# Another order of the weight loads in a two-layer diffusion block with 32 experts a layer

## The chip, the core and the metric

The kernel runs on one core of a Trainium2 chip. Its engines are TensorE (PE, matrix products), VectorE (DVE), ScalarE (ACT), GpSimd (POOL) and SyncE (SP), which issues most of the transfers. The metric is the device time of one execution in microseconds, lower is better. All data is float32, all products are full float32 products.

## What is computed

Two layers over 256 latent tokens and 256 context tokens of width 1024. Each layer: a modulation vector from the conditioning (`silu(c) @ w_mod + b_mod`), a modulated RMS norm, one input projection split among four mixers (A a bidirectional mLSTM, B global attention, C windowed attention, D neighbourhood attention), a gated sum of the branches and an output projection; then a second norm and a mixture of 32 experts:

```python
def layer(x, l):
    h = rms_norm(x, norm1_g[l]) * (1 + sc1) + sh1
    y = sum(sigmoid(gate[i]) * (branch[i](h @ w_in[l]) @ w_branch[l, i]) for i in range(4)) @ w_out[l]
    x = x + ga1 * y
    t = rms_norm(x, norm2_g[l]) * (1 + sc2) + sh2
    expert, w = top2_in_best_group(sigmoid(t @ w_router))          # 2 of 32 for each token
    for e in range(32):                                            # tokens gathered by expert
        ys = (silu(xs @ e_gate[l, e]) * (xs @ e_up[l, e])) @ e_down[l, e]
    return x + ga2 * scatter_add(w * ys)
```

In layer 1 only the latent tokens go on after the mixers. The result is a final RMS norm.

## The kernel before

Each layer runs through the same stages, with one set of buffers. SBUF holds a ring of six slots of 2 MB (`ring`); slots 0 to 2 take the weights of the dense part in turn, slots 3 to 5 (`ext`) hold operands and results of the dense part and become slots for experts later. A plan written out ahead (`plan_dense`) numbers every dense product group; `dense_full` counts them, and a transfer into a slot waits for the number of the group that used the slot last. `blocks[l]` is the list of a layer's dense weight transfers, sorted by when their slot comes free; SP issues them in that order from one queue, each behind its wait.

**Start of a layer.** Four row blocks of `w_mod` (2 MB each, order `MOD_ORDER`) give shift and scale of the first norm: `modulation_parts(n)`, then `modulation_row(n)` on TensorE, evacuated by ScalarE (`part_evac`, `mod_evac`). Before, the blocks go to slots 0, 1, 2 and again 0, so that the fourth waits for the first product. The tokens (`X`, two transfers of 1 MB) stand in SP's queue behind the third block. In layer 0 ScalarE's order is part 0, part 1, row 0, part 2, row 1, four squares of the tokens, root, part 3, rows 2 and 3. In layer 1 it is all parts and rows, then the scaling of the fetched expert outputs (`scale_first`) and the squares; DVE adds the outputs (`add_output`) behind that. The fetched outputs come by eight gathers on POOL's queue (`fetch_outputs`), after the last scatter of the experts has landed; two of the four token tiles go to the tensor HT.

**Mixers.** Stages A, D, B, C in this order. A stage has items (a pair of heads and a token tile); layer 1 has eight items a stage, so nine steps in D, B and C. Between the parts of an item TensorE does filling work, dealt to steps by `due(l, b, i)`: in D queries and keys for B, the output products of A (`value`) and the gates of D; in B the same for C. Before, `due` deals D, B and C by length (in layer 1 a query group counts 4, a key group 2, a value group 1, a gate group 2). The neighbourhood bias comes in two halves through one buffer: the second half is loaded by POOL after item 3 has used the first (`bias_used`), and item 4 needs it. DVE norms and turns B's queries and keys in `prepare_normed`, whose steps follow from the step of the last key group.

**Experts.** Expert e uses gate, up and down weights of 2 MB each. The ring holds two experts (slot 3 x parity + 0, 1, 2). Two more matrices are loaded ahead into memory that is free during the choice: the gate weights to HT after the last router product, the up weights to the first 4096 columns of `scr` after the last rank product. Before, these are those of the last expert, 31. SP issues in order: up and down of 1, gate, up and down of 0, gate of 1 (after the normed tokens are stored in DRAM), the two overlay loads, constants for the next layer (PICK, MODA, G1), and then in a loop gate, up and down of e + 2 as soon as expert e's product with the same slot is done (`g_full`, `u_full`, `y_full`). In layer 1 (`TILED`) an expert's down product runs after the next expert's gate and up products, and the queue's order is shifted to match. POOL gathers an expert's rows (`xe_full`) and scatters its results.

## Time and profile before

| | us |
|---|---|
| median of 3 runs | 2692.15 (2687.77 to 2692.79) |
| profiled execution | 2690.23 |
| its span | 2688.6 |
| TensorE busy | 2408.3 (90%) |
| DVE busy | 1025.4 (38%) |
| ScalarE busy | 501.5 (19%) |
| GpSimd busy | 230.8 (9%) |
| bytes moved | 614.75 MB, 229 GB/s over the span |
| chain of waits | TensorE 66%, DMA 23%, DVE 7% |

The chain of waits is followed back from the last instruction to whatever released each step; its shares say which engine or transfer held the end at each time. A group in the timeline carries in brackets the idle time ahead of it and what ended it. "Landing" is the time from the issue of a transfer to its semaphore. TensorE runs at one of two granted clocks, 1.2 or 2.4 GHz, shown as 0.5 or 1.0 (PEclk).

### The profile page before, as it was taken

Reading aid. Unit: us, or ns where it says so; the run is one execution under the profiler, and the core shown is the slowest. Engines: PE = TensorE matmul, PEld = TensorE weight load, DVE = VectorE, ACT = ScalarE, POOL = GpSimd, SP = SyncE. Lnnn points to the kernel's source line nnn. Section 1 sums busy time; section 2 is a strip of 40 time slices with the busy share of each in tenths; the row PEclk is TensorE's granted clock in tenths of the full one; section 3 lists DMA queues with packets and bytes.
Section 4 is the critical chain, followed back from the end, with each engine's and each line's share of the span. In section 5 each row is a group of like instructions: output and inputs, shape, how many; then the busy total and the mean of one; then the engine's idle time right before and its main releaser. Section 6 shows DMA issues by size and latency. Waiting matters only on the chain.

```text
span 2688.6 us, 45465 instructions
## 1 busy us (share of the span) xinstructions
PE 2408.3 (90%) x19016; PEld 1450.8 (54%) x19017; DVE 1025.4 (38%) x2392; ACT 501.5 (19%) x992; POOL 230.8 (9%) x392
## 2 busy tenths in 40 slices
PE   5999999999998979999999489999999788887884
PEld 2455545454444467777667156567676444444442
DVE  2226545365674332322222232435557521111112
ACT  2023222222231101111001112222223111101011
POOL 3000001000000011111110100000000011111111
PEclk8989999999999879999999798999999889999997
DMA  9111118234344479999999521133456779999993
GB/s 300 63 63 63 48 63 315 92 114 115 101 133 138 172 279 413 409 404 391 386 390 351 219 75 63 63 110 91 155 179 192 288 308 414 410 416 413 413 397 137
DMA packets 151925, 614.75 MB, mean 229 GB/s; under 512 B 16145, under 2 KB 20785, under 8 KB 135249
## 3 DMA queue, kind: packets, MB, share of 16 engines
q1 hardware_dynamic: 127138, 558.01, 54.5%
q0 software_dynamic: 24688, 55.39, 6.7%
q8 instruction: 66, 1.08, 0.2%
q14 instruction: 33, 0.27, 0.0%
HBM read 596.39 MB, written 42.11 MB: 237 GB/s over the span
## 4 chain that ended last, share of the span: by engine, by line
PE 66%; DMA 23%; DVE 7%; issue 2%; ACT 1%; POOL 0%; SPq 0%; DVEq 0%; POOLq 0%; ACTq 0%
DMA ring<-in_e_down_dram 21%; PE bank L1469 12%; PE bank L1349 11%; PE bank L1339 7%; PE bank L1733 5%; PE bank L1482 5%; PE score_banks L1750 4%; PE score_banks L1770 3%; PE bank L1640 2%; PE score_banks L1518 2%; PE bank L1542 2%; PE turned_banks L1528 2%; PE score_banks L1755 2%; PE bank L1726 2%; PE bank L1647 1%
## 5 line engine op out<-in xcount | busy, mean ns | idle before, releaser
L1469 PE MATMUL bank<-HT,ring 128*128 128x512 f32 (+1 forms) x1024 | 343.3, 490 | 0.4 <-ACT ring L1041 0.4
L1349 PE MATMUL bank<-ring,HT 128*128 128x512 f32 (+1 forms) x800 | 299.1, 530 | 0.0
L1733 PEld LDWEIGHTS bank<-scr,ring 128*64 128x64 f32 x7936 | 279.2, 138 | 15.5 <-issue 14.7
L1733 PE MATMUL bank<-scr,ring 128*64 128x80 f32 x7936 | 284.6, 234 | 2.1 <-DVE scr L2477 1.1
L1726 PE MATMUL bank<-ring,scr 128*64 128x256 f32 x1984 | 229.1, 384 | 40.7 <-DMA ring<-in_e_up_dram 20.1
L1469 PEld LDWEIGHTS bank<-HT,ring 128*128 128x128 f32 x1024 | 192.0, 192 | 124.0 <-issue 111.3
L1349 PEld LDWEIGHTS bank<-ring,HT 128*128 128x128 f32 x800 | 150.9, 192 | 133.8 <-issue 127.8
L1726 PEld LDWEIGHTS bank<-ring,scr 128*64 128x64 f32 x1984 | 140.2, 138 | 132.5 <-DMA ring<-in_e_gate_dram 37.2
L1339 PE MATMUL bank<-HT,ring 128*128 128x512 f32 (+1 forms) x512 | 196.2, 542 | 1.9 <-ACT HT L1041 1.9
L1770 PE MATMUL score_banks<-ring,scr 128*64 128x512 f32 x512 | 135.3, 676 | 37.7 <-DMA ring<-in_e_down_dram 36.0
L1339 PEld LDWEIGHTS bank<-HT,ring 128*128 128x128 f32 x512 | 97.1, 192 | 92.0 <-issue 88.4
L1296 ACT ACT_TABLE_LOAD x64 | 82.1, 1283 | 327.7 <-DVE scr L2518 152.1
L1041 ACT ACTIVATE ring<-bank 128x512 f32<-128x512 f32 (+1 forms) x122 | 62.4, 522 | 418.1 <-PE bank L1469 218.2
L1296 ACT ACTIVATE scr<-bank 128x320 f32<-128x320 f32 (+1 forms) x64 | 26.3, 411 | 604.9 <-PE bank L1733 321.8
L1750 PE MATMUL score_banks<-ring,scr 128*64 128x512 f32 x512 | 125.4, 635 | 14.4 <-DMA ring<-in_e_down_dram 13.6
L2129 DVE SCALAR_TENSOR_TENSOR scr<-ring,csil,scr 128x512 f32<-128x512 f32 x160 | 112.8, 747 | 0.6 <-DMA ring<-in_w_mod_dram 0.3
L2495 DVE TENSOR_TENSOR scr<-scr,bank 128x320 f32<-128x320 f32 x32 | 15.6, 488 | 242.2 <-PE bank L1733 242.2
L1213 ACT ACTIVATE scr<-turned_banks 128x1024 f32<-128x1024 f32 (+1 forms) x72 | 63.5, 882 | 208.8 <-PE turned_banks L1528 208.8
L2483 DVE COPY scr<-score_banks 64x512 f32<-64x512 f32 x64 | 44.0, 687 | 149.9 <-PE score_banks L1770 149.4
L1224 ACT ACTIVATE scr<-score_banks,nms 128x512 f32<-128x512 f32 (+1 forms) x144 | 87.0, 609 | 72.6 <-DVE nms L2270 72.6
L1770 PEld LDWEIGHTS score_banks<-ring,scr 128*64 128x64 f32 x512 | 41.6, 153 | 107.2 <-issue 88.7
L1482 PE MATMUL bank<-ring 128*128 128x512 f32 (+1 forms) x256 | 89.2, 497 | 5.6 <-DVE ring L2101 5.6
(277 smaller groups left out, 2678.7 us busy)
## 6 DMA issues: line engine op xcount, KB each, us to landing
ring<-in_e_down_dram SPq DMA_DIRECT2D x64, 2048.0 KB, 26.5
ring<-in_e_up_dram SPq DMA_DIRECT2D x62, 2048.0 KB, 27.8
ring<-in_e_gate_dram SPq DMA_DIRECT2D x62, 2048.0 KB, 27.5
ring<-in_w_in_dram SPq DMA_DIRECT2D x34, 2048.0 KB, 8.6
ring<-in_w_mod_dram SPq DMA_DIRECT2D x32, 1024.0 KB, 5.1
ring<-in_w_mod_dram SPq DMA_DIRECT2D x8, 2048.0 KB, 17.0
ys<-consts POOLq DMA_DIRECT2D x1, 10240.0 KB, 35.8
ring<-in_w_branch_dram SPq DMA_DIRECT2D x4, 2048.0 KB, 7.8
```

The lines of the kernel that those rows point to most:

```text
L1213: act.activation(PTP[:, :, 0:w], PT_[:, :, 0:w], ACT.Copy).then_inc(pair_pt, 1)
L1224: last = act.activation(PB[:, hf, 0:512 - lo], SP_[:, hf, lo:512], ACT.Exp, bias=nms[:, at + hf:at + hf + 1], scale=0.125, accum_out=rsum[ ...
L1296: act.activation(SE[:, 0:hw], ps[2][:, 0:hw], ACT.Silu).then_inc(sg_ready, 1)
L1339: m = pe.matmul(bank[:, 0:cols], w[:, k, j * P:j * P + P], HT[:, k, 0:cols], start=k == 0, stop=k == KT_D - 1)
L1349: m = pe.matmul(bank[:, 0:width], HT[:, k, t * P:t * P + P], w[:, k, 0:width], start=k == 0, stop=k == KT_D - 1)
L1469: m = pe.matmul(bank[:, 0:NQ], w[:, k, (ft % 4) * P:(ft % 4) * P + P], HT[:, k, 0:NQ], start=k == 0, stop=k == KT_D - 1)
L1482: m = pe.matmul(bank[:, 0:NQ], wb[:, k, ft * P:ft * P + P], OT[b][:, k, 0:NQ], start=k == 0, stop=k == 3)
L1726: m = pe.matmul(ps[bank][hf * HALF:hf * HALF + cap, 0:256], XTv[:, k, :], w[:, k, hf * 256:hf * 256 + 256], start=k == 0, stop=k == KT_D - 1)
L1733: m = pe.matmul(ps[bank][rows_, f * cap:f * cap + cap], w[:, k, f * P + hf * HALF:f * P + hf * HALF + HALF], XTv[:, k, :], start=k == 0, s ...
L1750: m = pe.matmul(ps[4][hf * HALF:hf * HALF + HALF, :], hv[:, f, 0:HALF], w[:, f, hf * 512:hf * 512 + 512], start=f == 0, stop=f == 3)
L1770: m = pe.matmul(ps[4][hf * HALF:hf * HALF + HALF, :], lhs, w[:, f, hf * 512:hf * 512 + 512], start=f == 0, stop=f == 3)
L2129: m = dve.scalar_tensor_tensor(out=acc, in0=x, scalar=c, in1=acc, op0=ALU.mult, op1=ALU.add)
```

## The change

- The two overlay buffers take gate and up of expert 1 instead of 31. SP's order becomes: up of 2, down of 1, expert 0's three, gate of 1 (overlay), gate of 2, the constants, up of 1 (overlay, after the first gather has landed), then gate and up of 3 and down of 2 behind expert 0, down of 3, and a loop from 4 on. Ring slots of gate and up are thereby shifted by one expert: the last even expert ends in slots 3 and 4, the last odd one in 0 and 1.
- The four row blocks of a layer's start go to slots 3, 4, 2, 0, the first projection block (mq) to slot 1, all free without a product of the same layer. In layer 1, SP waits for all gathers of the outputs ahead of the fifth block.
- The tokens are loaded by ScalarE's queue, after its first activation.
- `due` deals the groups of layer 1's stages D and B by number instead of by length.

```diff
@@ -216,10 +216,9 @@
 def due(l, b, i):
 
     steps, n = stage_steps(l, b), len(fill_groups(l, b))
-    if b == "A":
+    if b == "A" or (l == L - 1 and b != "C"):
         return range(n * i // steps, n * (i + 1) // steps)
-    last = l == L - 1
-    length = {"val": 1, "gat": 2, "gq": 4 if last else 2, "wq": 4 if last else 2, "gkv": 2 if last else 1, "wkv": 2 if last else 1}
+    length = {"val": 1, "gat": 2, "gq": 2, "wq": 2, "gkv": 1, "wkv": 1}
     size = [length[name[:3]] for name, _ in fill_groups(l, b)]
     at = [sum(size[:k]) * steps // sum(size) for k in range(n)]
     return range(sum(1 for a in at if a < i), sum(1 for a in at if a <= i))
...
@@ -579,8 +578,9 @@
 
         for l in range(L):
             qt = q_tiles(l)
-            expert = EXPERTS * l - 1
-            user = [(-2, (s, v) if l else None) for s, v in ((g_full, expert), (u_full, expert), (y_full, 2 * expert))]
+            done = EXPERTS * l
+            user = [(-2, (s, v) if l else None) for s, v in ((g_full, done), (u_full, done), (y_full, 2 * done - 2),
+                                                         (g_full, done - 1), (u_full, done - 1))]
             todo = []
 
...
@@ -623,7 +623,7 @@
 
             for n in range(4):
                 at = 512 * MOD_ORDER[n]
-                add_block((l, "mod", n), kview(w_mod, at, at + 512), 512, "mod_p", n + 1)
+                add_block((l, "mod", n), kview(w_mod, at, at + 512), 512, "mod_p", n + 1, (3, 4, 2, 0)[n])
             for name, n in (("mq", 4), ("mk", 4), ("mv", 4), ("mo", qt), ("nq", 4), ("nk", 4), ("nv", 4)):
                 add_in(name, n)
             add_gates("A")
@@ -719,12 +719,12 @@
                 for at, (dst, src, wait, arrived) in enumerate(blocks[l]):
                     if wait:
                         sp.wait_ge(*wait)
+                    if l and at == 4:
+                        for t in range(4):
+                            sp.wait_ge(yg_full[t], 32 * l)
                     sp.dma_start(dst, src).then_inc(arrived, 16)
                     if (l, at) == (0, 0):
                         sp.dma_start(PICK, ins["consts"][:, N_CONST + N_LATE:]).then_inc(pick_loaded, 16)
-                    if (l, at) == (0, 2):
-                        sp.dma_start(X[0:HALF, :, :], ins["x"][0].rearrange("(t p) d -> p t d", p=HALF)).then_inc(x_loaded, 16)
-                        sp.dma_start(X[HALF:P, :, :], ins["ctx"][0].rearrange("(t p) d -> p t d", p=HALF)).then_inc(x_loaded, 16)
 
                 def load_expert(c, e, par):
 
@@ -736,23 +736,17 @@
                     sp.dma_start(slot_view(3 * par + c, 512 if c < 2 else D), src).then_inc(w_full[3 * par + c], 16)
 
                 sp.wait_ge(mg_done, 32 * (l + 1))
-                for c in (1, 2):
-                    load_expert(c, 1, 1)
+                load_expert(1, 2, 1)
+                load_expert(2, 1, 1)
                 for (s, v), slot in last_users[l]:
                     sp.wait_ge(s, v)
                     load_expert(slot, 0, 0)
                 sp.wait_ge(dense_full, G[l, "h2t", 7] + 1)
+                sp.wait_ge(dense_full, G[l, "router", 3] + 1)
+                sp.dma_start(SECOND_GATE, ins["e_gate"][l, 1].rearrange("(p k) n -> p k n", p=P)).then_inc(second_gate_loaded, 16)
                 sp.wait_ge(h2_stored, 64 * (l + 1))
-                load_expert(0, 1, 1)
-
-                def whole(name):
-
-                    return ins[name][l, EXPERTS - 1].rearrange("(p k) n -> p k n", p=P)
-
-                sp.wait_ge(dense_full, G[l, "router", 3] + 1)
-                sp.dma_start(LAST_GATE, whole("e_gate")).then_inc(last_gate_loaded, 16)
-                sp.wait_ge(dense_full, G[l, "rank", 2] + 1)
-                sp.dma_start(LAST_UP, whole("e_up")).then_inc(last_up_loaded, 16)
+                load_expert(0, 2, 1)
+
                 sp.wait_ge(dest_ready, l + 1)
                 if l + 1 < L:
                     sp.dma_start(PICK, ins["consts"][:, N_CONST + N_LATE:]).then_inc(pick_loaded, 16)
@@ -762,42 +756,36 @@
                     sp.dma_start(G1, ins["final_g"].partition_broadcast(P)).then_inc(next_loaded, 16)
 
                 eb = l * EXPERTS
+                sp.wait_ge(dense_full, G[l, "rank", 2] + 1)
+                sp.wait_ge(xe_full[0], 8 * eb + 16)
+                sp.dma_start(SECOND_UP, ins["e_up"][l, 1].rearrange("(p k) n -> p k n", p=P)).then_inc(second_up_loaded, 16)
+
+                def load_hidden(after, e, par):
+
+                    sp.wait_ge(g_full, eb + after + 1)
+                    load_expert(0, e, par)
+                    sp.wait_ge(u_full, eb + after + 1)
+                    load_expert(1, e, par)
+
+                def load_down(after, e, par):
+
+                    sp.wait_ge(y_full, 2 * (eb + after + 1))
+                    load_expert(2, e, par)
+
+                load_hidden(0, 3, 0)
+                load_down(0, 2, 0)
                 if not TILED[l]:
-                    def reload(i, j, hidden_too):
-
-                        if hidden_too:
-                            sp.wait_ge(g_full, eb + 2 * i - 1 + j)
-                            load_expert(0, 2 * i + j, j)
-                            sp.wait_ge(u_full, eb + 2 * i - 1 + j)
-                            load_expert(1, 2 * i + j, j)
-                        sp.wait_ge(y_full, 2 * (eb + 2 * i - 1 + j))
-                        load_expert(2, 2 * i + j, j)
-
-                    with sp.Fori(1, EXPERTS // 2 - 1) as i:
+                    load_down(1, 3, 1)
+                    with sp.Fori(2, EXPERTS // 2) as i:
                         for j in range(2):
-                            reload(i, j, True)
-                    reload(EXPERTS // 2 - 1, 0, True)
-                    reload(EXPERTS // 2 - 1, 1, False)
+                            load_hidden(2 * i + j - 2, 2 * i + j, 1 - j)
+                            load_down(2 * i + j - 2, 2 * i + j, j)
                 else:
-
-                    def refill(e, par, down_too, hidden_too=True):
-
-                        if hidden_too:
-                            sp.wait_ge(g_full, eb + e + 1)
-                            load_expert(0, e + 2, par)
-                            sp.wait_ge(u_full, eb + e + 1)
-                            load_expert(1, e + 2, par)
-                        if down_too:
-                            sp.wait_ge(y_full, 2 * (eb + e))
-                            load_expert(2, e + 1, 1 - par)
-
-                    refill(0, 0, False)
-                    with sp.Fori(0, EXPERTS // 2 - 2) as i:
+                    with sp.Fori(2, EXPERTS // 2) as i:
                         for j in range(2):
-                            refill(2 * i + 1 + j, 1 - j, True)
-                    refill(EXPERTS - 3, 1, True, False)
-                    sp.wait_ge(y_full, 2 * (eb + EXPERTS - 2))
-                    load_expert(2, EXPERTS - 1, 1)
+                            load_hidden(2 * i + j - 2, 2 * i + j, 1 - j)
+                            load_down(2 * i + j - 3, 2 * i + j - 1, 1 - j)
+                    load_down(EXPERTS - 3, EXPERTS - 1, 1)
...
             act.activation(csil[:, :, :], craw[:, :, :], ACT.Silu).then_inc(csil_ready, 1)
+            act.dma_start(X[0:HALF, :, :], ins["x"][0].rearrange("(t p) d -> p t d", p=HALF)).then_inc(x_loaded, 16)
+            act.dma_start(X[HALF:P, :, :], ins["ctx"][0].rearrange("(t p) d -> p t d", p=HALF)).then_inc(x_loaded, 16)
...
+                def hidden_weights(i, j, c):
+
+                    if isinstance(i, int) and (i, j) == (0, 1):
+                        pe.wait_ge((second_gate_loaded, second_up_loaded)[c], 16 * (l + 1))
+                        return (SECOND_GATE, SECOND_UP)[c]
+                    if isinstance(i, int) and (i, j) == (0, 0):
+                        return expert_weights(pe, l, c, 0, 512)
+                    return expert_weights(pe, l, 3 * (1 - j) + c, i - 1 + j, 512)
...
                 gathered_turn(0, 8 * eb + 16, eb + 1)
                 if TILED[l]:
                     tiled(0, 0, False, True)
-                    with pe.Fori(0, EXPERTS // 2 - 1) as i:
+                    tiled(0, 1, True, True)
+                    tiled(1, 0, True, True)
+                    with pe.Fori(1, EXPERTS // 2 - 1) as i:
                         tiled(i, 1, True, True)
                         tiled(i + 1, 0, True, True)
...
                 else:
-                    with pe.Fori(0, EXPERTS // 2 - 1) as i:
+                    for j in range(2):
+                        expert(0, j, True)
+                    with pe.Fori(1, EXPERTS // 2 - 1) as i:
                         for j in range(2):
                             expert(i, j, True)
```

## Rows read from the trace of the kernel before

**Rows 1.** the page's 40 slices: what all DMA engines moved

```profile
GB/s 300 63 63 63 48 63 315 92 114 115 101 133 138 172 279 413 409 404 391 386 390 351 219 75 63 63 110 91 155 179 192 288 308 414 410 416 413 413 397 137
```

**Rows 2.** chain of waits, layer 0's experts: start us, length us, what

```profile
1186.38 27.05 DMA ring<-in_e_down_dram
...
1440.43 27.23 DMA ring<-in_e_down_dram
```

**Rows 3.** chain of waits, layer 1's experts

```profile
2228.07 26.36 DMA ring<-in_e_down_dram
...
2611.56 26.03 DMA ring<-in_e_down_dram
```

**Rows 4.** timeline of SP's queue, layer 0: start us, us, engine, line, operation

```profile
954.30 0.33 SPq L755 DMA_DIRECT2D scr<-in_e_up_dram  x1
...
973.09 0.35 SPq L736 DMA_DIRECT2D ring<-in_e_gate_dram  x1
...
1000.54 0.38 SPq L736 DMA_DIRECT2D ring<-in_e_down_dram  x1
```

**Rows 5.** chain of waits, layer 0's choice of experts

```profile
956.01 6.81 DMA scr<-h,idx_all
```

**Rows 6.** tile view of idx_all, 950 to 1000: landing of the gathers

```profile
DMA to landing us min/median/max: 3.5/6.1/6.8
```

**Rows 7.** DMA issues of 1441 to 1458: KB, median us to landing

```profile
ring<-in_e_down_dram SPq DMA_DIRECT2D x1, 2048.0 KB, 15.4
```

**Rows 8.** timeline, all engines, end of layer 0 and start of layer 1

```profile
1487.81 1.92 PE L1755 MATMUL score_banks<-ring,scr 128*16 128x256 f32 x32
...
1497.28 0.96 POOL L973 DMA_INDIRECT scr<-ys,dest_i  x1 [4.05 <-issue]
...
1519.25 3.64 PE L1378 MATMUL bank<-ring,scr 128*32 128x512 f32 x16 [11.34 <-issue]
...
1528.34 2.18 ACT L1047 ACTIVATE scr<-scr,wn 128x1024 f32<-128x1024 f32 x2
```

**Rows 9.** timeline of TensorE: both hidden products of one expert, layer 0

```profile
1457.24 9.07 PE L1733 MATMUL bank<-scr,ring 128*64 128x80 f32 x256
```

**Rows 10.** timeline, all engines, start of layer 0

```profile
24.70 2.70 PE L1378 MATMUL bank<-ring,scr 128*32 128x512 f32 x16 [1.02 <-issue]
...
34.62 1.06 ACT L1070 ACTIVATE scr<-X 128x1024 f32<-128x1024 f32 x1 [3.60 <-DMA X<-in_ctx_dram]
...
39.81 3.37 PE L1378 MATMUL bank<-ring,scr 128*32 128x512 f32 x16 [9.43 <-issue]
...
40.64 4.87 DVE L1950 SCALAR_TENSOR_TENSOR scr<-X,small,scr 128x1024 f32<-128x1024 f32 x4
...
48.16 4.63 DVE L1956 TENSOR_TENSOR scr<-scr 128x1024 f32<-128x1024 f32 x4 [2.64 <-ACT scr L1041]
```

**Rows 11.** windows of the start: busy per engine, PEclk, DMA share, GB/s

```profile
10.00:15.00 5.00, 3.64 (x16) 0.68 (x16) 0.00 (x0) 0.60 (x1) 1.11 (x2) 1.00 1.06 391
...
25.00:30.00 5.00, 5.00 (x20) 1.10 (x12) 0.00 (x0) 0.60 (x1) 0.00 (x0) 0.66 1.02 214
```

**Rows 12.** timeline of SP's queue, start of layer 1's experts

```profile
2174.22 0.33 SPq L736 DMA_DIRECT2D ring<-in_e_gate_dram  x1
...
2192.14 0.38 SPq L736 DMA_DIRECT2D ring<-in_e_down_dram  x1
```

**Rows 13.** timeline, all engines, last expert of layer 1

```profile
2645.03 3.67 PE L1726 MATMUL bank<-scr 128*64 128x256 f32 x32
...
2654.14 3.65 PE L1770 MATMUL score_banks<-ring,scr 128*64 128x512 f32 x16 [1.63 <-DVE scr L2512]
```

**Rows 14.** timeline of DVE, stage D of layer 1

```profile
1837.73 2.34 DVE L2253 SCALAR_TENSOR_TENSOR scr<-scr,consts 128x384 f32<-128x384 f32 x4 [5.46 <-DMA scr<-in_n_rel_bias_dram]
```

**Rows 15.** timeline of TensorE, stage D of layer 1

```profile
1845.34 5.22 PE L1482 MATMUL bank<-ring 128*128 128x256 f32 x16 [5.62 <-DVE ring L2101]
...
1886.84 2.82 PE L1399 MATMUL bank<-consts,scr 128*128 128x128 f32 x12 [2.06 <-DVEq L2220]
```

28 lines of the change are left out of this document (8 added, 20 removed).

## The prediction

> **What bounds the kernel now.** I read the 40 slices of the page first [rows 1]: the core moves about 410 GB/s in two plateaus, the expert stages of layer 0 (about 965 to 1490 us) and layer 1 (2165 to 2658), and far less elsewhere. Then the chain of waits: in both plateaus it runs from one landing of down weights to the next. Between landings of experts 15 and 30 in layer 0 lie 254.2 us [rows 2], 15 experts of three 2 MB loads, so 5.65 us a load; in layer 1 landings of experts 5 and 29 give 383.1 us over 72 loads, 5.32 us [rows 3]. An expert stage thus ends when a fixed count of loads has run through, and what counts is when the stream starts to run without holes, and what TensorE still has to do when the last load is there. Outside these plateaus the chain is TensorE's, but for two spots: the start of each layer, where the row blocks of w_mod are waited for, and stage D of layer 1.
>
> **Edit 1, the second expert's gate and up in the overlay instead of the last one's.** Both kernels hold eight of 96 loads when expert 0 runs, so 88 remain; only their order and the last overlay load change.
> (a) The up load into the overlay was issued at 954.30 [rows 5], ahead of the first gather, which took 6.81 us; the quickest of the first three gathers took 3.5 [rows 6, 4]. Now it waits for that gather. The bus is not empty (G1, PICK and the second gather are there), so the gather saves between 0 and 3.3 us; I take 2.3. The overlay load lands within some 8 us of 961, before expert 1's up at about 985, so it is hidden; uncovered it would cost TensorE a wait of one load, 5.65. Queued on SP behind this wait are only waits of the expert stage, the first of them at 973 [rows 5].
> (b) The stream in layer 0. Before, g2, u2, d2, g3, u3, d3 are issued from 973.09, every 4 to 7 us, so it is full from the start: the 87th load, expert 30's down, landed at 1467.66, and 1467.66 - 87 x 5.65 = 976.1, 3.0 after that issue [rows 2, 5]. After, g3, u3 and d2 follow expert 0, but expert 1 gives no ring slot back except down: d3 waits for y(1), issued at 1000.54 before [rows 5], 998.2 now. Three loads from 973 are through by about 990, so **the bus stands idle about 10 us** before it runs full. Then 85 loads: 998.2 + 3.0 + 85 x 5.65 = 1481.5 for the last landing, against 1457.4 + 15.4 = 1472.8 before (the down load of 1441 to 1458) [rows 7]. The stream ends 8.7 us later.
> (c) The tail. Before, the last load is expert 31's down while its gate and up products still have to run: TensorE ended at 1489.7 [rows 8], 16.9 behind the landing. After, gate and up weights of 31 land 11.3 and 5.65 ahead of the down weights, their products (9.07 us for the two) fit [rows 9], and 3.65 + 1.92 = 5.6 remain: 1487.1. Net gain 2.6, so the 8.7 is more than paid back, barely.
> (d) Layer 1. The stream restarts without holes at d2, which waits for y(0): 2192.14 - 2.5 = 2189.6 [rows 12]. Expert 29's down, the 86th load, landed 2637.58, that is 5.8 behind 2174.22 + 86 x 5.32 [rows 3, 12]. Up of 31 is now the 84th load from the restart: 2189.6 + 5.8 + 84 x 5.32 = 2642.3, down of 30 at 2647.6, down of 31 at 2652.9. With 3.7 for a product and the 2 us of turning and copying before the last one, the last product starts at 2653.2, against 2654.14 [rows 13]; with layer 0's offset of 3.0 in place of 5.8 it is 2650.4. Gain 1 to 4, **I take 2**.
>
> **Edit 2, the row blocks of layer 1 in four free slots, the fifth block held for the gathers.** Before, the fourth block waited for the first block's product, was issued at 1499.93 and was there at 1519.25, and 9.1 us later ScalarE, which evacuates that row first, began to scale tokens at 1528.34 [rows 8]; DVE's sums, the transposes and TensorE's projections hang on that. After, the four blocks follow the stream directly: four loads after 1481.5 is 1504.1. The gathers of the outputs (POOL, from 1497.28 [rows 8], about the same now: TensorE ends 2.6 earlier but the last scatter shares a full bus) move 8 x 512 KB, as much as two loads, 11.3 us. So the fourth block is there between 1504.1 and 1515.4. Before, it took 19.3 from issue to landing among the same gathers [rows 8], so it gets the smaller share, and I take 1513: **-6**, from -15 to -4. This contains the 2.6 of (c), which nobody else waits for. The hold of block five on the gathers keeps mq, mk and mv queued on SP; mq is issued near 1516 and needed when the last transposes are done, 30 us later; if the cover were gone, a load each.
>
> **Edit 3, the start.** The same slots let four blocks and mq be issued at once; the tokens leave SP's queue, where they stood behind block three, for ScalarE's, at about 3.4 us. Block three was there at 24.70, tokens at 34.62, block four at 39.81 [rows 10]. While the tokens (two transfers to 64 partitions each) were moving the bus gave 214 GB/s, against 391 with blocks alone [rows 11]. All of this still has to be moved before block four, which stays near 39.8 (35 if the two kinds fill each other's gaps). But ScalarE squares the tokens only after it evacuates block three's row, and now that block lies behind the tokens: it lands between 24.6 + 2.1 MB / 391 GB/s = 30.0 and 34.6. From block to evacuated row 6.3 us (24.70 to 31.0), from first square to the end of DVE's scaling 10.9 (34.62 to 45.5): DVE is done at 47.2 to 51.8, where the next step began at 48.16 [rows 10]. **Cost -1 to +4, I take +3**, nearer to serial. POOL's waits for block one move some 5 us later; their data is wanted at 49 and later.
> The Trainium skill ("SBUF — State Buffer", the section on the DMA port swizzle) says that 64 partitions reach only half of the ports, about 218 GB/s; the 214 agrees. It also says ("DMA: Bandwidth & Descriptors", Issuing engines are not separate DMA queues) that transfers of several issuers interleave on the same 16 engines and save issue time alone; by this block three would land at 34.6 and the edit cost nearly 4.
>
> **Edit 4, D and B of layer 1 by number.** TensorE has the same products; only stalls move. In D it waits 5.62 us at 1845.34 because the second half of the bias, loaded after the fourth item, lands at 1837.7, and 2.06 at 1886.84 for the last normed key tile [rows 14, 15]. By number, two more groups (3.5 + 1.9 us) stand ahead of the fourth item and the bias comes 5.3 later, but less value work is left to cover it: stall 7.3. The norm is spread over three steps instead of two, which removes the second stall and 0.8 beside it. **Net -1**; it could be +4 if the norm is late all the same, -4 if both stalls shrink. In B wk and the value weights are needed earlier but land 5 us or more ahead.
>
> **Sum**: +3 - 6 - 1 - 2 = -6. The profiled execution took 2690.23 (span 2688.6), so 2684.2; the median of the three runs lies 1.9 above it: 2692.15 - 6 = **2686.2**.
>
> **Rivals.** *R1, the bus was the whole cost at both starts:* tokens and blocks fill each other's gaps (start 0), block four lands at 1505 (-14), layer 1's tail gives 4. About -18, 2674. For it: 391 against 214 GB/s; against: 19.3 us for block four among the gathers. *R2, the gathers take the bus:* block four no earlier than before, since the last gathers now meet three queued blocks: start +3, switch -1, D/B -1, tail -1: 0, 2692. For it again the 19.3. *R3, slower: the hole in the stream.* Place: between d2 and d3 of layer 0 and g3 and d2 of layer 1. I price it at 8.7 in the first; each further microsecond delays every later landing by one. If the stream ends 15 us later instead of 8.7 and likewise 6 in layer 1, the switch gives 0 and layer 1's tail costs 4: +3 + 0 - 1 + 4 = +6, 2698. It decides from a shift of about 14 us. Against it: expert 1's down is only 15 us behind expert 0's. *R4, the edit of D does not do what it says* (stalls grow by 4): -1, 2691, counted with R2.
>
> **How the numbers follow.** Less than 0.2% (5.4 us) cannot be told from no change. Forecast 0.45 (its own range 2682 to 2690; 0.26 of it beyond the bound, 0.19 inside), R1 0.23 faster, R2 with R4 0.18 same, R3 0.14 slower. Faster 0.49, same 0.37, slower 0.14. The range reaches from R1 to short of R3: 2674 to 2696.
>
> **What would show it.** Right: a hole in the bus's windows near 990 to 1000 and last landing near 1481; TensorE's end near 1487; the fourth block's product at 1513 and ScalarE's scaling at 1522; DVE's second pass at the start near 51; in D one stall of 7 instead of 5.6 + 2. Wrong: no hole (then the gain is 8 more), the fourth block at 1505 or at 1519, the start at 48, last product of layer 1 later than 2654 relative to its stage's start.

## The result, and the profile after

The changed kernel takes 2670.72 us (median of 5, 2668.15 to 2679.63) against 2691.57 for the kernel before beside it. The ratio is 0.9929, with a 95% interval of 0.9912 to 0.9947: 0.7% faster, 21 us by the medians. The forecast was 2686.2, a change of -6, and the time lies below its range of 2674 to 2696. Its profiled execution has a span of 2666.6 us.

I cut both traces at the same products of TensorE: first projection product of layer 0 ("start"), first expert product, end of layer 0's last down product, first projection of layer 1, first scores of D, first scores of B, first expert product of layer 1, last down product, end.

| stretch, us | before | after | change | forecast |
|---|---|---|---|---|
| start | 55.83 | 58.86 | +3.0 | +3 |
| dense part and choice, layer 0 | 909.71 | 908.88 | -0.8 | -2.3 |
| experts, layer 0 | 524.19 | 522.30 | -1.9 | -0.3 |
| switch of layers | 71.08 | 57.93 | **-13.1** | -3.4 |
| A, layer 1 | 227.69 | 227.41 | -0.3 | 0 |
| D, layer 1 | 110.84 | 101.86 | **-9.0** | -1 (with B) |
| B, C and choice, layer 1 | 269.06 | 267.37 | -1.7 | 0 |
| experts, layer 1 | 485.74 | 488.30 | +2.6 | -2 (with the line below) |
| end | 34.46 | 33.69 | -0.8 | |

(The forecast put -6 on the end of the switch, 2.6 of it won by the end of layer 0; here it is split so. From the start to that point, the measured change is -15.9.) Two stretches carry all 22 us. The page's first section and its slices of what the DMA engines moved, of after; the columns of the first line are busy time, its share of the span and the instructions:

```profile
PE 2397.7 (90%) x19016; PEld 1448.3 (54%) x19017; DVE 1025.3 (38%) x2392; ACT 500.9 (19%) x992; POOL 231.6 (9%) x392
...
GB/s 302 63 64 51 46 46 295 111 146 98 109 125 133 146 249 383 408 402 404 390 378 397 306 87 64 63 111 91 166 186 208 272 290 410 414 415 414 413 411 155
```

The same 19016 matmuls keep TensorE busy for 10.6 us less than before, and its mean granted clock rose from 0.947 to 0.955: part of what a stall costs is booked behind it, in products at the lower clock. In D, TensorE is idle for 2.2 us instead of 8.5 and its busy time falls by 2.7 (granted clock 0.98 instead of 0.94). In the switch it is idle for 34.1 us instead of 43.4 and busy for 3.9 less (0.71 instead of 0.64).

**Start.** Timeline of all engines, after, the lines that answer [rows 10] (start, length, engine, line, operation, idle time before):

```profile
17.71 3.64 PE L1368 MATMUL bank<-ring,scr 128*32 128x512 f32 x16 [17.71 <-DMA ring<-in_w_mod_dram]
...
35.12 1.92 PE L1368 MATMUL bank<-ring,scr 128*32 128x512 f32 x16
...
39.68 1.05 ACT L1060 ACTIVATE scr<-X 128x1024 f32<-128x1024 f32 x1
...
40.43 1.92 PE L1368 MATMUL bank<-ring,scr 128*32 128x512 f32 x16 [1.28 <-issue]
...
50.61 4.63 DVE L1941 TENSOR_TENSOR scr<-scr 128x1024 f32<-128x1024 f32 x4
```

Block three's product is at 35.1 (24.70 before), block four's at 40.4 (39.81), DVE's second pass at 50.6 (48.16). The cost came as worked out.

**Layer 0's stream.** Windows of 5 us, after: busy time of PE, PEld, DVE, ACT and POOL (instructions in brackets), PEclk, DMA share, GB/s. The bus stands still where it was forecast to, and in windows of 1 us it shows 0 to 16 GB/s from 994 to 1002:

```profile
990.00:995.00 5.00, 4.54 (x120) 4.29 (x117) 0.10 (x1) 0.13 (x1) 0.00 (x0) 1.00 0.63 236
995.00:1000.00 5.00, 5.00 (x36) 2.11 (x39) 1.81 (x4) 1.28 (x1) 0.00 (x0) 1.00 0.00 0
1000.00:1005.00 5.00, 5.00 (x134) 4.27 (x128) 2.53 (x6) 0.00 (x0) 2.02 (x4) 1.00 0.50 154
```

**Switch.** Timeline of all engines, after, against [rows 8]:

```profile
1484.53 3.65 PE L1740 MATMUL score_banks<-ring,scr 128*64 128x512 f32 x16 [1.04 <-DMA ring<-in_e_down_dram]
1488.12 1.92 PE L1745 MATMUL score_banks<-ring,scr 128*16 128x256 f32 x32
...
1500.81 0.97 POOL L961 DMA_INDIRECT scr<-ys,dest_i  x1 [7.27 <-issue]
...
1509.28 1.93 PE L1368 MATMUL bank<-ring,scr 128*32 128x512 f32 x16
...
1515.95 2.17 ACT L1035 ACTIVATE scr<-scr,wn 128x1024 f32<-128x1024 f32 x2
```

The last landing, near 1484.5, lies 516.8 us behind the first expert product at 967.74 (forecast 518.3). The fourth block's product no longer waits: it starts at 1509.28 behind other products, at the full clock (1.93 us; 3.64 before), and the scaling follows 6.7 us later (9.1 before). What is left of the waiting lies ahead of the first two blocks' products: 5.46 and 1.41 us of idle time before 1495.50 and 1501.36.

**D of layer 1.** Timeline of TensorE, after, against [rows 15]: the stalls of 5.62 and 2.06 are now

```profile
1830.54 1.13 PE L1508 MATMUL score_banks<-ring 64*128 64x512 f32 x4 [1.82 <-ACT scr L1214]
...
1865.49 7.14 PE L1459 MATMUL bank<-HT,ring 128*128 128x256 f32 x32 [0.38 <-ACT scr L1029]
```

### The profile page after: what moved, and what is told of

Same layout as the page of the kernel before. It is cut to its first block, busy times and chain, and to the rows that moved or that the text cites. A ratio compares the mean times of both kernels' runs of the same rounds, so it can differ in the third digit from the quotient of the medians.

```text
span 2666.6 us, 45449 instructions
## 1 busy us (share of the span) xinstructions
PE 2397.7 (90%) x19016; PEld 1448.3 (54%) x19017; DVE 1025.3 (38%) x2392; ACT 500.9 (19%) x992; POOL 231.6 (9%) x392
## 4 chain that ended last, share of the span: by engine, by line
PE 66%; DMA 24%; DVE 6%; issue 2%; ACT 1%; POOL 0%; SPq 0%; DVEq 0%; POOLq 0%; ACTq 0%
DMA ring<-in_e_down_dram 23%; PE bank L1459 12%; PE bank L1339 12%; PE bank L1329 7%; PE bank L1723 5%; PE bank L1472 5%; PE score_banks L1740 3%; PE score_banks L1760 3%; PE bank L1630 2%; PE score_banks L1508 2%; PE turned_banks L1518 2%; PE bank L1532 2%; PE bank L1716 2%; PE score_banks L1745 2%; PE bank L1637 1%
## 5 line engine op out<-in xcount | busy, mean ns | idle before, releaser
L1760 PE MATMUL score_banks<-ring,scr 128*64 128x512 f32 x512 | 133.5, 669 | 38.6 <-DMA ring<-in_e_down_dram 37.0
L1740 PE MATMUL score_banks<-ring,scr 128*64 128x512 f32 x512 | 121.7, 619 | 16.8 <-DMA ring<-in_e_down_dram 16.7
```

Source lines behind the costliest of these rows:

```text
L1740: m = pe.matmul(ps[4][hf * HALF:hf * HALF + HALF, :], hv[:, f, 0:HALF], w[:, f, hf * 512:hf * 512 + 512], start=f == 0, stop=f == 3)
L1760: m = pe.matmul(ps[4][hf * HALF:hf * HALF + HALF, :], lhs, w[:, f, hf * 512:hf * 512 + 512], start=f == 0, stop=f == 3)
```

## The experiments

Each was timed beside the kernel before. The table gives the median, the ratio to before with its interval, and the stretches of its profile ("dense 0" is the dense part and choice of layer 0, "to exp. 1" is B, C and choice of layer 1; A and the end are left out). Between the two profiles of the changed kernel (after, e14) a stretch differs by up to 3 us, so groups are compared, not single cells.

| kernel | median | ratio | start | dense 0 | exp. 0 | switch | D | to exp. 1 | exp. 1 |
|---|---|---|---|---|---|---|---|---|---|
| before | 2691.6 | 1 | 55.8 | 909.7 | 524.2 | 71.1 | 110.8 | 269.1 | 485.7 |
| after | 2670.7 | 0.9929 (0.9912-0.9947) | 58.9 | 908.9 | 522.3 | 57.9 | 101.9 | 267.4 | 488.3 |
| e14, after once more | 2672.0 | 0.9933 (0.9919-0.9947) | 60.2 | 909.3 | 524.8 | 60.8 | 101.9 | 267.4 | 488.7 |
| e1, D and B by length | 2679.8 | 0.9961 (0.9948-0.9974) | 60.4 | 909.2 | 522.5 | 58.0 | 110.6 | 265.4 | 486.6 |
| e2, e1 + gate block held | 2672.3 | 0.9928 (0.9914-0.9943) | 61.4 | 909.1 | 524.4 | 59.0 | 101.3 | 267.6 | 488.8 |
| e3, tokens on SP | 2665.8 | 0.9906 (0.9892-0.9921) | 56.2 | 907.9 | 523.8 | 59.0 | 100.6 | 265.8 | 486.5 |
| e4, before + edit 2 | 2677.8 | 0.9948 (0.9935-0.9961) | 57.5 | 910.1 | 524.8 | 56.9 | 108.9 | 271.0 | 486.0 |
| e5, no hold | 2671.2 | 0.9921 (0.9907-0.9936) | 58.6 | 908.8 | 524.1 | 61.4 | 101.9 | 267.5 | 488.2 |
| e6, up not behind the gather | 2678.4 | 0.9952 (0.9938-0.9965) | 59.6 | 909.7 | 522.5 | 59.1 | 101.9 | 273.6 | 486.9 |
| e7, before + edit 1 | 2679.3 | 0.9951 (0.9938-0.9965) | 58.1 | 908.8 | 525.2 | 62.1 | 110.6 | 265.5 | 485.7 |
| e9, before + edits 2, 4 | 2669.7 | 0.9916 (0.9902-0.9929) | 57.7 | 911.0 | 525.7 | 58.2 | 100.6 | 269.1 | 483.2 |
| e10, e9 + up of 31 behind the gather | 2664.8 | 0.9901 (0.9887-0.9915) | 58.0 | 908.8 | 524.1 | 56.0 | 101.9 | 267.4 | 484.2 |
| e11, e3 + B by length | 2667.8 | 0.9910 (0.9895-0.9925) | 56.8 | 908.8 | 523.2 | 59.2 | 101.9 | 268.0 | 488.3 |
| e12, tokens on two queues | 2666.3 | 0.9910 (0.9897-0.9924) | 54.0 | 908.6 | 523.7 | 61.5 | 101.8 | 267.5 | 486.2 |
| e13, e3 + gate block held | 2668.0 | 0.9912 (0.9899-0.9925) | 58.0 | 908.7 | 522.7 | 58.0 | 101.9 | 267.5 | 488.3 |
| e15, before + hold | 2690.5 | 0.9999 (0.9990-1.0008) | 55.9 | 910.0 | 525.3 | 69.7 | 109.0 | 271.0 | 483.7 |
| e16, fourth block held | 2686.0 | 0.9983 (0.9974-0.9992) | 60.6 | 909.3 | 523.8 | 73.6 | 101.9 | 267.4 | 489.6 |
| e17, e10 + tokens on two queues | 2661.2 | 0.9896 (0.9881-0.9911) | 53.8 | 907.6 | 525.6 | 57.7 | 100.7 | 265.7 | 484.1 |

### D: e1, e2 and e13

e1, the dealing undone:

```diff
-    if b == "A" or (l == L - 1 and b != "C"):
+    if b == "A":
...
+    last = l == L - 1
-    length = {"val": 1, "gat": 2, "gq": 2, "wq": 2, "gkv": 1, "wkv": 1}
+    length = {"val": 1, "gat": 2, "gq": 4 if last else 2, "wq": 4 if last else 2, "gkv": 2 if last else 1, "wkv": 2 if last else 1}
```

> The changed kernel with D and B of layer 1 dealt by length again, all else kept. Reading of the two traces: D lasts 101.9 us from its first scores to those of B, against 110.8 before, so the dealing is worth 9 us, not the 1 of the forecast. If so: 2670.7 + 9 = 2679.7, in D a stall near 5.6 ahead of a value product, the second half of the bias landing 9 to 10 us after its last issue, and a stall near 2 ahead of the norm's turning. Rival, the forecast's own term: the dealing gives 1 us, and D is shorter for another reason (a transfer that the new slots moved): 2671.7, with D still at 102 to 103 us.

Measured: 2679.8, D 110.6, a stall of 5.45: the first theory. e2 adds to it, in SP's loop over the blocks (17 is D's second gate block):

```diff
+                    if l and at == 17:
+                        sp.wait_ge(bias_loaded, 128 * (2 * l + 2))
```

> As the kernel with dealing by length, but SyncE issues the second block of D's gate weights only after the second half of the bias has landed; that block is needed some 35 us later. Theory 'bias meets gate block': dealt by length, the group that frees the slot ends 3 us after the bias is issued, so 2 MB share the bus with the bias; without them it lands 4 to 5 us after its last issue, the stall of 5.6 shrinks to under 1.5, the stall ahead of the norm stays near 2, and the time falls by 4 to 6 against dealing by length: 2674 to 2676. Rival 'work order': the stall of 5.6 is there because too little work stands behind the fourth item, and the landing is slow by itself: no change against dealing by length, 2679.7, landing still 9 to 10 us.

Measured: 2672.3 and D 101.3, without touching the order of the products. Timelines of e1: SP's issue of the gate block, POOL's eight issues of the bias, DVE's use of it, TensorE's stall.

```profile
1815.79 0.37 SPq L726 DMA_DIRECT2D ring<-in_w_in_dram  x1
...
1812.44 5.15 POOL L853 DMA_DIRECT2D scr<-in_n_rel_bias_dram  x8 [272.23 <-DVEq L2249]
...
1826.57 2.34 DVE L2239 SCALAR_TENSOR_TENSOR scr<-scr,consts 128x384 f32<-128x384 f32 x4 [5.29 <-DMA scr<-in_n_rel_bias_dram]
...
1834.17 2.04 PE L1473 MATMUL bank<-ring 128*128 128x256 f32 x4 [5.45 <-DVE ring L2087]
```

The same of e2, with TensorE's second stall as the last line:

```profile
1825.62 0.37 SPq L728 DMA_DIRECT2D ring<-in_w_in_dram  x1
...
1816.76 5.15 POOL L855 DMA_DIRECT2D scr<-in_n_rel_bias_dram  x8 [273.21 <-DVEq L2251]
...
1833.46 2.83 PE L1475 MATMUL bank<-ring 128*128 128x256 f32 x12 [0.43 <-DVE ring L2089]
...
1873.44 1.53 PE L1392 MATMUL bank<-consts,scr 128*128 128x128 f32 x12 [2.05 <-DVEq L2208]
```

In e1 the gate block is issued 3.4 us behind the first of the bias's transfers, and the bias is there 14.1 us after that first issue (1826.57 - 1812.44). In e2 the gate block goes only when the bias is there, at 1825.62, 8.9 us after its first issue. Before, the two numbers are the same as in e1: the bias is issued from 1823.43, the gate block at 1826.78, and the bias is there at 1837.73 [rows 14], 14.3 later. Timelines of before, POOL and SP:

```profile
1823.43 3.21 POOL L864 DMA_DIRECT2D scr<-in_n_rel_bias_dram  x5 [272.94 <-DVEq L2263]
...
1826.78 0.37 SPq L722 DMA_DIRECT2D ring<-in_w_in_dram  x1
```

In the changed kernel the last key group runs one step earlier, so the gate block leaves at 1810.55, 5.1 ahead of the bias (1815.63), and the bias is there at 1824.47, 8.8 later. The counts by queue show the sharing. From 1820 to 1822 the queue of the bias (q0) moved 0.30 MB alone on the bus in e2, and 0.13 MB beside the gate block (q1) in e1, whose counts are:

```profile
q1 hardware_dynamic: 202, 0.41, 72.5%
q0 software_dynamic: 61, 0.13, 27.5%
```

So the dealing pays because it takes one 2 MB transfer out of the bias's way. The norm's stall of 2.05 stays in e2, and D is as short as with the dealing by number. What is left is small: e2's 2672.3 against 2670.7 and 2672.0 for the changed kernel.

e13 is e3 (below) with the same hold.

> The changed kernel with tokens on SyncE's queue, both stages by number, and the second block of D's gate weights held until the second half of the bias has landed. By number that block is issued 5 us ahead of the bias and overlaps only its first microseconds; one stall of 1.75 us is left in D. Theory 'the rest of the stall is still bus': the bias lands 1 to 2 us earlier, the stall goes, D 98.9 instead of 100.6: 2664. Rival 'the rest is DVE's and ScalarE's work on the item': no change, 2665.8.

Measured 2668.0 with D at 101.9 and the stall still 1.78: no gain. The bias takes 8.8 us from its first issue to its use here too (1817.99 to 1826.80), so a gate block 5 us ahead of it costs it nothing. What is left of the stall in D isn't the gate block.

### Tokens: e3 and e12

e3, the tokens back on SP's queue behind the third block:

```diff
+                    if (l, at) == (0, 2):
+                        sp.dma_start(X[0:HALF, :, :], ins["x"][0].rearrange("(t p) d -> p t d", p=HALF)).then_inc(x_loaded, 16)
+                        sp.dma_start(X[HALF:P, :, :], ins["ctx"][0].rearrange("(t p) d -> p t d", p=HALF)).then_inc(x_loaded, 16)
...
-            act.dma_start(X[0:HALF, :, :], ins["x"][0].rearrange("(t p) d -> p t d", p=HALF)).then_inc(x_loaded, 16)
-            act.dma_start(X[HALF:P, :, :], ins["ctx"][0].rearrange("(t p) d -> p t d", p=HALF)).then_inc(x_loaded, 16)
```

> The changed kernel with the tokens back on SyncE's queue behind the third row block, the fourth and the first projection block behind them without a wait. Theory 'tokens delay every row block': block one's product starts near 10 instead of 17.7 and block three's near 25 instead of 35; the first projection product starts at 55.8 or earlier instead of 58.9, so 2670.7 - 3 = 2667.7, down to 2666.5 if the 1.2 us that the dense part of layer 0 lost besides comes back too. Rival 'the bytes are the same': all four blocks and the tokens have to be there in any order, first projection product at 58 to 59, 2670.7.

Measured 2665.8, 5 us faster than after by the medians. Over all profiles the start is 58.6 to 61.4 with the tokens on ScalarE's queue (after, e14, e1, e2, e5, e6, e16) and 55.8 to 58.1 on SP's (before, e3, e4, e7, e9, e10, e11, e13, e15); the means are 60.0 and 57.1. Edit 3 costs 3, the one part of the change that loses.

e12 leaves the latent tokens there and gives the context tokens to ScalarE's queue, behind `part_evac(1)`:

```diff
                 part_evac(1)
+                if l == 0:
+                    act.dma_start(X[HALF:P, :, :], ins["ctx"][0].rearrange("(t p) d -> p t d", p=HALF)).then_inc(x_loaded, 16)
                 mod_evac(0)
```

> The changed kernel with the latent tokens on SyncE's queue behind the third block and the context tokens on ScalarE's queue, issued after it has evacuated the second block's product, near 22 us. The first go to partitions 0 to 63, the second to 64 to 127. Theory 'one transfer to 64 partitions is what is slow (219 to 238 GB/s from 25 to 35), and two at once to different halves run at the full rate': 2.1 MB pass in 5.4 us instead of 10, block four's product at 35 to 36 instead of 40.2, the first projection product at 52 instead of 56.2: 2665.8 - 4 = 2661.8. Rival 'the rate belongs to the tokens however they are issued' (with tokens beside row blocks the bus gave 246 and 223 GB/s from 10 to 20): no window above 300 GB/s while tokens move, no change: 2665.8.

Windows from 25 to 35, first e3, then e12:

```profile
25.00:30.00 5.00, 4.87 (x19) 1.41 (x20) 0.00 (x0) 0.60 (x1) 0.00 (x0) 0.66 1.04 219
30.00:35.00 5.00, 0.81 (x2) 0.00 (x0) 1.23 (x1) 0.92 (x2) 0.00 (x0) 0.78 1.01 238
```

```profile
25.00:30.00 5.00, 5.00 (x20) 1.04 (x12) 0.00 (x0) 0.60 (x1) 0.00 (x0) 0.75 1.02 287
30.00:35.00 5.00, 0.02 (x1) 0.00 (x0) 1.23 (x1) 2.80 (x6) 0.00 (x0) 0.59 1.03 321
```

The counts by queue separate the tokens from block four. From 24 to 32 both queues carry tokens in e12, and behind that SP's queue carries block four alone. From 26 to 28 and 28 to 30 the engines moved 307 and 299 GB/s in e12, 203 and 229 in e3. The queues of e12 from 26 to 28 (q10 is ScalarE's):

```profile
q1 hardware_dynamic: 78, 0.32, 53.8%
q10 hardware_dynamic: 72, 0.29, 49.5%
```

Two transfers to different halves of the partitions, issued from two queues, run faster together than one alone, but not at the 390 of the blocks. Block four's product is at 37.9 (40.2 in e3) and the start at 54.0: half of what the theory wanted. Its median, 2666.3, doesn't show it, and its profile has a long switch (61.5). The Trainium skill ("SBUF — State Buffer", the section on the DMA port swizzle) gives about 218 GB/s for 64 partitions; the 219 agrees.

### Slots: e4, e7, e9, e15, e16, e5

e4, the kernel before with edit 2 alone:

```diff
-            user = [... for s, v in ((g_full, expert), (u_full, expert), (y_full, 2 * expert))]
+            user = [... for s, v in ((g_full, expert), (u_full, expert), (y_full, 2 * expert), (g_full, expert - 1), (u_full, expert - 1))]
...
+                add_block((l, "mod", n), kview(w_mod, at, at + 512), 512, "mod_p", n + 1, (3, 4, 0, 2)[n])
```

> The kernel before with edit 2 alone: four row blocks in slots 3, 4, 0, 2, the fifth block held for the gathers of the outputs; the overlay still takes expert 31, the tokens and the dealing are as before. Theory 'the free slots are the whole gain of the switch': with the last down load landing at 1472.8 four loads more are through by 1496, ahead of the gathers that start at 1497; the scaling starts near 1515 instead of 1528.3 and the time is 2691.6 - 13 = 2678.6, down to 2675. Rival 'the other expert order carries it': TensorE's end 2.6 us earlier and the saved gather make part of the gain, edit 2 alone gives the forecast's 6: 2685.6. In layer 1's start nothing else should move, and the last product should lie as far behind the first expert's as before.

Measured 2677.8, the switch 56.9. The free slots bring all 14 us of the switch without edit 1, as the first theory had it. e7 is the reverse, edit 1 alone (edits 2 to 4 undone):

> The kernel before with edit 1 alone (the second expert's gate and up in the overlay), row blocks in slots 0, 1, 2, 0, tokens on SyncE's queue, dealing by length. With it slots 0 and 1 are freed by expert 31's products, the last ones, instead of 30's, so the first two row blocks of layer 1 leave some 9 us later than before. Theory 'edit 1 is a wash by itself': first product 2 us earlier in each layer, stream 4 to 9 later, tail as forecast: 2691.6 - 4 to 2691.6 + 4, centre 2690. Rival 'edit 1 alone costs': the row blocks stand behind the tail and the gathers, the fourth product at 1525 or later: 2697.

Measured 2679.3, 8 us below the lower edge of the first theory, so both missed; the switch alone is 9.0 shorter, and the way to layer 1's first expert 3.6. Timelines of e7, SP, POOL and TensorE, show why:

```profile
1502.12 0.37 SPq L723 DMA_DIRECT2D ring<-in_w_mod_dram  x1
...
1502.17 0.96 POOL L962 DMA_INDIRECT scr<-ys,dest_i  x1 [6.60 <-issue]
...
1514.12 2.79 PE L1367 MATMUL bank<-ring,scr 128*32 128x512 f32 x12 [3.28 <-issue]
```

The fourth block still waits for the first product, but the last scatter now shares a full bus and lands later (POOL waits 6.6 ahead of the gathers instead of 4.05 [rows 8]; the bus moves 398 and 381 GB/s from 1490 to 1500, before 35 and 34), so the block's issue and the first gather meet. Before, the first gather was 2.6 us ahead of the block. The product follows the issue by 12.0 here, by 19.3 there. SP's issue of the fourth block in before:

```profile
1499.90 0.37 SPq L722 DMA_DIRECT2D ring<-in_w_mod_dram  x1
```

The counts by queue show where most of the 7 us go. Beside the gathers (q0) the blocks' queue (q1) gets the smaller share in both kernels, here before from 1508 to 1510:

```profile
q0 software_dynamic: 144, 0.52, 64.8%
q1 hardware_dynamic: 145, 0.30, 38.2%
```

In e7 the block has the bus to itself before the gathers' data starts (from 1504 to 1506 q1 moves 0.72 MB, q0 nothing), and some 6 us behind its issue q1 (the block, and mq behind it) has moved 1.35 MB, against 0.68 before. At 0.147 MB a us, the pace beside the gathers, the difference is worth 4.6 us, an estimate from these counts. The other 2.7 are not settled.

Two edits remove the same wait, so their gains, 12.9 and 13.4, don't add. With both and the dealing, e3 is 25.0 below before; with edit 2 and the dealing alone, e9 is 23.0 below.

> The kernel before with edits 2 and 4, without 1 and 3: it differs from the changed kernel with tokens on SyncE's queue (2665.8) by edit 1 alone. Theory 'effects add': 2677.8 (edit 2 alone) - 9 (edit 4) = 2668.8, so edit 1 is worth 3: 2 from the first gather of layer 0, 3 from that of layer 1, less 2 to 3 at the tail of layer 1. Rival 'edit 1 loses in the streams what it wins at the gathers': 2665.8, the same as with it. In D of layer 1 100.6 to 102 us in either case.

Measured 2669.7: edit 1 is worth 2 to 4 on top of edit 2 (medians, and the ratios 0.9916 and 0.9906). The intervals overlap; the stretches, over all kernels, are firmer (next section).

e15 is the kernel before with the hold alone, e16 the changed kernel with the hold one block earlier:

```diff
+                    if l and at == 4:
+                        for t in range(4):
+                            sp.wait_ge(yg_full[t], 32 * l)
```

```diff
-                    if l and at == 4:
+                    if l and at == 3:
```

> The kernel before with the hold alone: row blocks in slots 0, 1, 2 and again 0, and SyncE waits for the gathers of the outputs ahead of the fifth block. Theory 'mq and mk crowd the fourth block': before, 7.7 MB went over the bus from 1500 to 1520 and the fourth block was there at 1519.25; with only the gathers' 4.2 MB and its own 2.1 beside each other from 1497.3 it is there by 1497.3 + 6.3 MB / 395 GB/s = 1513.3, the scaling starts near 1522.5, and the time is 2691.6 - 5.5 = 2686. Rival 'the gathers alone hold it': it stands behind them whatever follows, 1518 to 1519, 2691.6.

> The changed kernel with the hold one block earlier, so that the fourth row block of layer 1 too is issued only after all gathers have landed. Theory 'the free slot pays because the block goes ahead of the gathers': the gathers land some 11 us after 1500.8, the fourth block 6 to 8 us after that, its product at 1518 to 1520 instead of 1509.3, the scaling near 1526: 2670.7 + 9 to 10 = 2680, and nearly all of the gain of the switch is gone. Rival 'the gathers bind': alone on the bus they land earlier and the sums are done earlier, which pays for the late row: within 3 us of 2670.7.

Timelines, first e15 (SP's issue of the fourth block, first gather, product), then e16 (issue and product):

```profile
1500.68 0.37 SPq L725 DMA_DIRECT2D ring<-in_w_mod_dram  x1
...
1498.44 0.96 POOL L976 DMA_INDIRECT scr<-ys,dest_i  x1 [3.68 <-issue]
...
1519.85 1.94 PE L1381 MATMUL bank<-ring,scr 128*32 128x512 f32 x8 [11.41 <-issue]
```

```profile
1518.91 0.37 SPq L725 DMA_DIRECT2D ring<-in_w_mod_dram  x1
...
1526.86 3.54 PE L1368 MATMUL bank<-ring,scr 128*32 128x512 f32 x16 [16.16 <-issue]
```

Taking mq and mk away (e15) changes nothing, 2690.5; my theory there falls and its rival holds. Putting the block behind the gathers (e16) costs 14 us against e14, timed beside it (15 against after), more than the 9 to 10 I gave, and undoes the whole gain of the switch (73.6). I had let the gathers land 11 us after the first one's issue; it took 15.4 (1503.50 to the block's issue at 1518.91). **What the free slots buy is a place ahead of the gathers.**

e5, the changed kernel without the hold:

> The changed kernel without the wait for the gathers ahead of the fifth block of layer 1, all else kept, so that 2 MB of mq share the bus with the gathers. Theory 'the gathers of the outputs hold the switch': the scaling starts when row products are done (1516), but DVE's sums want all four fetched tiles; with mq beside them the last gather lands about one load, 5.3 us, later, and the first projection product at 1551 to 1553 instead of 1548: 2674. Rival 'row blocks hold it': the rows are evacuated at 1515 whatever the gathers do, no change: 2670.7. A third case, mq's early landing being of use, gives at most 0 since mq was there before the transposes.

Measured 2671.2. The profile has a longer switch (61.4, the scaling 28.1 behind the end of layer 0's experts instead of 25.9), the medians show nothing. But this isn't the theory: it had the scaling stay and the gathers bind behind it. The longer switch comes ahead of the second block's product, which waits 2.36 and runs at the lower clock (1.41 and the full clock in after). e14, which has the hold, shows the same (2.40, a switch of 60.8). And in all 18 profiles TensorE idles for 26.23 to 26.25 us between the last row product and the transposes, with the hold and without it: the last row product sets the transposes, the gathers don't. Timelines of TensorE, after, then e5:

```profile
1541.66 5.36 PE L1389 MATMUL bank<-consts,scr 128*128 128x128 f32 x32 [26.25 <-DVE scr L1941]
```

```profile
1545.32 6.67 PE L1386 MATMUL bank<-consts,scr 128*128 128x128 f32 x32 [26.24 <-DVE scr L1938]
```

No run shows a gain of the hold; by the medians and their intervals it is worth at most some 3 us.

### The gather's wait: e6 and e10

e6, the changed kernel without `sp.wait_ge(xe_full[0], 8 * eb + 16)`:

> The changed kernel with the up weights of the second expert issued without waiting for the first gather of either layer (the last rank product alone releases them), so that 2 MB share the bus with the gather as before. Theory 'the load takes the gather's time': the gathers take 6.8 and 7.8 us again instead of 4.9 and 4.3, TensorE's first expert product comes 2 us later in layer 0 and up to 3.4 in layer 1. In layer 0 the end of the experts is set by the stream (restart at d3, behind y(1)), so the 2 us go through in full: sum +2 to +5, 2673 to 2676. Rival 'the stream has slack': the first expert's start moves, the last landing doesn't: 2670.7.

Measured 2678.4, above both theories. The way from B to the first expert of layer 1 takes 273.6 us instead of 267.4. Landings of the first gathers in layer 1, tile view of idx_all, first after, then e6, then before:

```profile
DMA to landing us min/median/max: 3.9/4.1/4.3
```

```profile
DMA to landing us min/median/max: 2.7/9.8/10.7
```

```profile
DMA to landing us min/median/max: 2.7/7.3/7.8
```

So e6 is more than a step back to before: its gathers are slower than before's too, and it overstates what the wait is worth.

e10 takes from edit 1 the wait alone. It is e9 with the overlay's up weights, still expert 31's, moved:

```diff
-                sp.wait_ge(dense_full, G[l, "rank", 2] + 1)
-                sp.dma_start(LAST_UP, whole("e_up")).then_inc(last_up_loaded, 16)
...
                 eb = l * EXPERTS
+                sp.wait_ge(xe_full[0], 8 * eb + 16)
+                sp.dma_start(LAST_UP, whole("e_up")).then_inc(last_up_loaded, 16)
```

> The kernel before with edits 2 and 4 (2669.7), and the overlay's up weights, still those of expert 31, issued only after the first gather has landed, behind the constants. It takes from edit 1 the wait alone and leaves the order of the experts. Theory 'edit 1 pays by its wait and costs by its order': the stretches up to the first expert product shorten by 1.3 in layer 0 and 3.2 in layer 1 (the means over the kernels with and without the wait), the last down product of layer 1 stays 483 to 486 us behind the first expert product: 2669.7 - 4.5 = 2665.2. Rival 'the order pays too' (it lets layer 0's experts end 1.4 earlier): the wait alone gives less, and what it brings in layer 0 is lost behind the last landing: 2668 or more.

Measured 2664.8, the first theory's value (2665.2): the new order of experts isn't needed for edit 1's gain.

### e11, e14, e17

> The changed kernel with tokens on SyncE's queue (2665.8), D dealt by number and B by length again. From the first scores of B to the first expert product of layer 1, kernels with B by length took 265.4 and 265.5, those by number 265.8 to 267.6 (all with the wait for the gather). Theory 'B by number costs 1 to 2': 2664.5. Rival 'B doesn't care': 2665.8. D stays at 100.6 to 102 in both.

Measured 2667.8, nearer to the rival, and to the first expert 268.0: the small cost of B by number that I read out of two profiles was scatter.

> The changed kernel once more, beside the other three on one chip: 2670.7 within 0.1%, and a second profile of it: start 58.6 to 61, last product of layer 0's experts to first projection of layer 1 57.9 to 59.1, D 101.9.

Measured 2672.0; start, D and the tail repeat, the switch is 60.8, outside what I gave, from the second block's product as in e5. A claim below 3 us from one profile needs a second.

e17 is e10 with e12's tokens.

> The order of experts of before, the overlay's up weights (expert 31) behind the first gather, four row blocks in slots 3, 4, 0, 2 with the hold, D and B by number (2664.8 so far), and the context tokens on ScalarE's queue after the second block's product. Theory 'the two queues give the 2 us that their profile shows at the start' (first projection product at 54.0, kernels with the tokens on one queue 55.8 to 58.1): 2662.8. Rival 'the start's gain is within its scatter', as the median of the run with two queues says (2666.3 against 2665.8): 2664.8.

Measured **2661.2, 30 us below before and 9.5 below the changed kernel** by the medians (intervals 0.9881 to 0.9911 and 0.9912 to 0.9947), with the start at 53.8. The parts that paid add up. Both profiles with two queues have the shorter start (54.0 and 53.8, all others 55.8 or more); that the time gains by it is not shown, since the intervals of e10 and e17 overlap and e12's median is no lower than e3's.

## Why the prediction was wrong

The kind of each effect in the start, the hole, the switch and D was right. Two terms were mis-sized, the switch and D, both by what shares the bus with a waited-for transfer, and a third was put at nothing: the lower clock behind a stall. The working cites rows 4 and 5 the wrong way round (the issues are in rows 4, the gather of 6.81 in rows 5), and its issue at 1499.93 is at 1499.90 in the timeline; neither moves the sum.

- **Start, +3: right**, and for the stated reason.
- **Hole in layer 0's stream: right** (0 GB/s from 995 to 1000). From the first expert product to the end it gave 523.9; measured 522.3. Kernels with edit 1 took 522.3 to 525.2, those without 524.1 to 525.7; their means differ by 1.4. The rival R3 didn't come.
- **Gathers: smaller than forecast in layer 0, left out in layer 1.** The first expert product came 0.8 earlier relative to the start in this profile, 1.4 in the means of the kernels with the wait and those without (2.3 forecast). I gave layer 1 nothing; there the way from B to the first expert product is 266.9 in the mean with the wait and 270.0 without (e6 not counted), 3 us. The landings show why: 4.3 at most, 7.8 before.
- **Switch, -6: the step that failed is the choice of 1513 between 1504 and 1515.** I took the row nearest in place, 19.3 us among the gathers [rows 8], as the price of a block. But that block had been issued behind the first gathers. In the changed kernel SP had issued the fourth block by 1491.85, 9 us ahead of the first gather at 1500.81, and the blocks' queue moved almost nothing after 1504 (0.03 MB to 1506, 0.01 to 1508), before the gathers were through. Ordered by that lead the runs read: issued 2.6 and 2.2 behind the first gather (before, e15), the product is 19.3 and 19.2 after issue; level with it (e7), 12.0; ahead of it (after, e4), nothing waits; behind all gathers (e16), 8.0, but the issue itself is only at 1518.9. My own bound of 1504 was the value to take. The gathers themselves were mis-sized too: I priced them at 11.3 us of bus, and alone on it they took 15.4 from first issue to the end of the hold (e16). And I took 9.1 us from product to scaling as fixed; without the stall the products run at the full clock and it is 6.7.
- **D and B, -1: the step "a stall of 7.3" failed.** I let the bias land a fixed time behind its trigger, 14.3 us. It was 8.8, as e1 and e2 show. The row I lacked was SP's: a gate block issued at 1826.78, in the middle of the bias. I also wrote that only stalls move; of the 9.0, 6.2 is idle time and 2.7 the same products at a higher granted clock. I had named each transfer's need, and not asked what else the dealing moves on SP's queue. B gave nothing, as forecast.
- **Tail of layer 1, -2: wrong sign.** It is +2.6 here; with edit 1 the stretch took 485.7 to 489.6, without it (before, e4, e9, e10, e15, e17) 483.2 to 486.0. Of the 3.5 between my 484.8 and the measured 488.3, the restart accounts for 2.3: d2 is issued at 2168.07, 23.5 us behind the first expert product, where I had 21.2. The rest is not settled.
- **The range** ended at R1's 2674. R1's switch was the true one, but R1 went with a start at 0 and D at -1; no case held a large gain in D, whose low end I had set at -4. 2692.15 + 3 - 14 (R1's switch) - 9 is 2672. R1's own terms, 0, -14, -1 and -4, add up to -19, where it says about -18.

## What to carry to other kernels

When a transfer is waited for, its price is not the row of the same transfer elsewhere but its place among what is on the bus: read the issue times of all queues around it, and ask which of them the change moves across it. A new dealing of work also moves the transfers that the work releases. Two edits that remove the same wait don't add, so time each alone; here the reordering of the experts, the largest part of the diff, brought what one moved wait brings.

## What was unexpected in the hardware

- A start 2.6 us ahead is enough: with the first gather that far ahead of the block, the block took 19.3 us from issue to product (19.2 in e15) instead of 12.0 (e7, one profile), though both are 2 MB beside the same 4 MB of gathers.
- The bias moves slowly even alone. From 1820 to 1822 in e2 its queue kept the DMA engines busy (100.7%) and moved 0.30 MB, 150 GB/s; with blocks alone they moved 391 [rows 11]. Windows of before, 1825 to 1830, most of it bias: busy at 0.99, 107 GB/s.

```profile
1825.00:1830.00 5.00, 5.00 (x36) 4.08 (x35) 2.44 (x7) 1.59 (x5) 3.57 (x6) 1.00 0.99 107
```

- An issue can itself be long. Timeline of SP's queue, after, the fourth row block, with the loads of the other row blocks issued just ahead of it (most issues take 0.33 to 0.39 us):

```profile
1484.43 7.42 SPq L725 DMA_DIRECT2D ring<-in_w_mod_dram  x1
```
